# Two transformer blocks on one core: the first feed-forward layer takes its norm behind the product, and modulation tiles are sent by the pace of the weight chunks

## The reference, cut to what matters

```python
def modulate_pre(x, g_pre, shift, scale):
    return rms_norm(x, g_pre) * (1.0 + scale[:, None, :]) + shift[:, None, :]
def gated_post_add(x, y, g_post, gate, weight):
    return x + weight * gate[:, None, :] * rms_norm(y, g_post)
def swiglu_ffn(h, w_in, w_out):
    g, u = jnp.split(h @ w_in, 2, axis=-1)
    return (jax.nn.silu(g) * u) @ w_out
# per layer:  mod = silu(c) @ ada_w[layer] + ada_b[layer];  at the very end: rms_norm_2(x, final_norm)
```

## Time and profile before

| what | value |
|---|---|
| median of 3 runs | 2206.66 us (2205.58 to 2207.31) |
| profiled execution, its time | 2205.55 us |
| its span on the core | 2203.6 us |
| PE / DVE / ACT / POOL busy | 2112.3 / 1579.0 / 1004.5 / 192.0 us |
| mean granted clock of TensorE | 0.977 |
| transfers | 497 MB, 226 GB/s over the span |

### The profile page before, as it was taken

The page is one execution under the profiler, slowest core; times in us unless marked ns, Lnnn a source line. Parts: engine busy times, 40 slices in busy tenths (PEclk is TensorE's granted clock), DMA queues, the critical chain, the costliest instruction groups (busy, mean ns, idle before and its releaser), DMA issues.

```text
span 2203.6 us, 39291 instructions
## 1 busy us (share of the span) xinstructions
PE 2112.3 (96%) x17014; PEld 2062.3 (94%) x17014; DVE 1579.0 (72%) x1945; ACT 1004.5 (46%) x1073; POOL 192.0 (9%) x326
## 2 busy tenths in 40 slices
PE   5999999999999998799999999999999999999997
PEld 5999999999999997599998999999999899998997
DVE  6777887886767776778878464758888545757655
ACT  3344545434534444644445463346445445335442
POOL 0111101111011100010101000001111000000000
PEclk8999999999889998999999999999999999999999
DMA  8899474996479953068975555465996655555652
GB/s 327 288 315 331 165 253 153 319 343 249 153 246 324 320 184 134 2 218 275 346 261 174 180 184 191 153 231 173 359 370 203 194 182 189 166 173 201 210 187 100
DMA packets 265388, 497.39 MB, mean 226 GB/s; under 512 B 17152, under 2 KB 146560, under 8 KB 264832
## 3 DMA queue, kind: packets, MB, share of 16 engines
q1 hardware_dynamic: 230192, 366.42, 49.7%
q0 software_dynamic: 35024, 128.47, 15.8%
HBM read 491.68 MB, written 1.05 MB: 224 GB/s over the span
## 4 chain that ended last, share of the span: by engine, by line
PE 81%; DVE 10%; DMA 4%; ACT 3%; issue 2%; SPq 0%; DVEq 0%; POOL 0%; ACTq 0%
PE PA L494 8%; PE PA L496 8%; PE PA L495 8%; PE PB L494 7%; PE PB L496 7%; PE PB L495 7%; PE PY L494 7%; PE PY L496 7%; PE PY L495 7%; DVE wlo L1352 3%; ACT whi L994 1%; DMA raw<-ffn_w_in 1%; DVE opA_lo L1437 1%; PE PY L525 1%; DMA raw<-w_ff 1%
## 5 line engine op out<-in xcount | busy, mean ns | idle before, releaser
L1352 DVE TENSOR_TENSOR wlo<-raw,whi 128x2048 fp32r<-128x2048 f32 x335 | 766.7, 2299 | 366.9 <-ACT whi L994 366.2
L994 ACT ACTIVATE whi<-raw 128x2048 fp32r<-128x2048 f32 x335 | 636.7, 1907 | 485.0 <-DMA raw<-ffn_w_in 202.5
L494 PE MATMUL PA<-opA_hi,whi 128*128 128x256 f32 x1344 | 381.1, 284 | 9.0 <-DVE opA_lo L1402 7.3
L494 PE MATMUL PY<-opB_hi,whi 128*128 128x256 f32 x1344 | 377.5, 281 | 4.6 <-DVE wlo L1352 3.9
L496 PE MATMUL PA<-opA_hi,wlo 128*128 128x256 f32 x1344 | 379.2, 282 | 0.0
L495 PE MATMUL PA<-opA_lo,whi 128*128 128x256 f32 x1344 | 378.1, 281 | 0.0
L496 PE MATMUL PY<-opB_hi,wlo 128*128 128x256 f32 x1344 | 375.8, 280 | 0.0
L495 PE MATMUL PY<-opB_lo,whi 128*128 128x256 f32 x1344 | 375.6, 279 | 0.0
L494 PE MATMUL PB<-opA_hi,whi 128*128 128x256 f32 x1216 | 343.0, 282 | 1.0 <-DVE wlo L1352 1.0
L496 PE MATMUL PB<-opA_hi,wlo 128*128 128x256 f32 x1216 | 342.0, 281 | 0.0
L495 PE MATMUL PB<-opA_lo,whi 128*128 128x256 f32 x1216 | 341.0, 280 | 0.0
(11 more groups left out here) (307 smaller groups left out, 3532.6 us busy)
## 6 DMA issues: line engine op xcount, KB each, us to landing
raw<-ffn_w_in SPq DMA_DIRECT2D x176, 512.0 KB, 5.3
scr<-adat POOLq DMA_DIRECT2D x154, 512.0 KB, 6.3
raw<-w_in SPq DMA_DIRECT2D x144, 512.0 KB, 4.6
raw<-w_ff SPq DMA_DIRECT2D x128, 512.0 KB, 4.6
raw<-ffn_w_out SPq DMA_DIRECT2D x88, 512.0 KB, 4.7
adaw<-adat POOLq DMA_DIRECT2D x86, 512.0 KB, 6.3
raw<-w_branch SPq DMA_DIRECT2D x48, 512.0 KB, 4.4
raw<-a_w_in SPq DMA_DIRECT2D x24, 512.0 KB, 4.4
```

What stands on the lines that cost most here:

```text
L494: nc.tensor.matmul(o_, w1, rhs(xh), start=start, stop=False, skip_group_check=True)
L994: AC(whi[slot][:, 0:w], raw[slot][:, 0:w], ACT.Copy).then_inc(hi_ready, 1)
L1352: TT(wlo[slot][:, 0:w], raw[slot][:, 0:w], whi[slot][:, 0:w].bitcast(F32), ALU.subtract).then_inc(lo_ready, 1)
```

## The change

1. ffn00 takes the z form (`ffn("ffn00", ..., True)`, `widened("00")`, zhi/zlo from x directly, `acc_x("00")` on POOL). The norm of x ahead of it (`ssq`, `squares`, `inverse("00.x")`) goes. ScalarE starts pre before chunk 1's copy.
2. SP's first transfers: c, tiles 0 and 1, vec, base, tiles 2 to 5, x, chunk 0, tiles 6 to 15, chunk 1. The silu table is loaded by a dummy before c is there. VectorE splits chunk 0 after 12 tiles.
3. POOL sends a modulation tile when TensorE has finished the chunk three places ahead of the one at which VectorE is to reduce it (`ada_with`, `ffn_due`, `ff2_due`), not when a buffer comes free; `acc_x` of a seam stands ahead of the sends of the next stage in POOL's order.
4. Tiles per stage: cmp 12 in place of 8 (four of them already after chunk 87's split), nsa 4 in place of 8. ffn00 and ffn10 begin with their tiles at the third place of their order in place of the first.
5. The tables of the attention stage (five transfers, 0.7 MB) are issued in ffn01 ahead of chunk 62, not after its last chunk.
6. Last norm: VectorE adds four squares, TensorE sums the other four directly; ScalarE forms x*gain in `t10`; VectorE multiplies pairs of tiles by the factor (four instructions in place of eight).

The core of the diff:

```diff
-("cmp", 0, 8), ("ffn10", 24, 40), ("nsa", 32, 8)
+("cmp", 0, 12), ("ffn10", 24, 40), ("nsa", 32, 4)
+        def ffn_due(name, p):
+            rn, a_ = RUN[name][1], 3 if name in ("ffn00", "ffn10") else 5
+            return min(rn, max(0, p - a_ + 1) * rn // (FFN_AT["in", FFN_STEPS - 1] - a_))
+        def ff2_due(name, p):
+            rn = RUN[name][1]
+            return min(rn, max(0, p - 5) * rn // (FF2_AT["out", FF2_STEPS - 2] - 6))
...
 SP:
-                    first_ada(range(0, 13))
+                    if name == "ffn01" and (kind, j) == ("in", 5):
+                        sp.wait_ge(multiplied, CH["conv_out"] + 4)
+                        sp.dma_start(tnsa, I["t_nsa"]).then_inc(nsa_in, 16)
+                        sp.dma_start(pos2, I["cmp_pos2"]).then_inc(cmp_in, 16)
...
-                                first_ada(range(13, 16))
+                                first_ada(range(6, 16))
...
+            sp.dma_start(crow[:], I["c_rows"][0:1].partition_broadcast(P)).then_inc(crow_in, 16)
+            first_ada(range(0, 2))
             sp.dma_start(vec[:], I["vec"]).then_inc(vec_in, 16)
             sp.dma_start(base[:], I["t_base"]).then_inc(base_in, 16)
+            first_ada(range(2, 6))
             sp.dma_start(x[:], I["x_fm"]).then_inc(x_in, 16)
...
 TensorE:
                     need(pe, "V", "fin.acc")
                     nc.tensor.matmul(PB[:, 0, :], onesD, accx[:], start=True, stop=False)
+                    for k in range(4, KT):
+                        need(pe, "S", f"fin.sq{k}")
+                        last = nc.tensor.matmul(PB[:, 0, :], onesD, tmp8[:, k, :], start=False, stop=k == KT - 1)
...
-            ssq("00.x")
-            for f in range(9, 16):
+            for f in range(8, 17):
                 pe.wait_ge(ada_used, f)
                 idle(6)
             need(pe, "V", "first.mod")
-            idle(14)
-            ffn("ffn00", "00", False)
+            idle(8)
+            ffn("ffn00", "00", True)
...
 ScalarE:
+                    for k in range(KT):
+                        if k == 4:
+                            root("fin")
+                        S(AC(t10[:, k, :], x[:, k, :], ACT.Copy, scale=V("final", k, 1)), f"fin.g{k}")
...
+            S(AC(warm[:], epsc[:], ACT.Silu))
             act.wait_ge(crow_in, 16)
             S(AC(crow[:], crow[:], ACT.Silu), "csil0")
+            load_table(ACT.Sqrt)
+            prep_to(1)
             act.wait_ge(x_in, 16)
-            squares("00.x", x, lambda q: None)
-            root("00.x")
-            prep_to(2)
-            pre("00", tmp8)
+            need(act, "V", "first.mod")
+            for k in range(KT):
+                S(AC(oph["A"][:, k, :], x[:, k, :], ACT.Copy, scale=A_("00")[:, k:k + 1]), f"00.zhi{k}")
+                if k == 3:
+                    prep_to(2)
+            for k in range(KT):
+                S(AC(tmp8[:, k, :], x[:, k, :], ACT.Square), f"00.sq{k}")
+            prep_to(3)
...
 VectorE:
             for f in range(16):
-                if f == 9:
-                    inverse("00.x")
-                if f == 13:
+                if f == 12:
                     prep_to(1)
                 ada_to(f + 1)
             mods("first")
+            widened("00")
+            for k in range(KT):
+                need(dve, "S", f"00.zhi{k}")
+                S(STT(opl["A"][:, k, :], x[:, k, :], A_("00")[:, k:k + 1], oph["A"][:, k, :].bitcast(F32), ALU.mult, ALU.subtract),
+                  f"00.zlo{k}")
+                if k == 3:
+                    prep_to(2)
...
+            ada_to(RUN["cmp"][0] + 4)
...
-            ada_to(nsa0 + 2)
...
-            ada_to(nsa0 + 4)
...
-                    for k in range(KT):
-                        S(STT(tmp8[:, k, :], x[:, k, :], V("final", k, 1), rstd[:], ALU.mult, ALU.mult), f"fin.t{k}")
+                    for q in range(4):
+                        need(dve, "S", f"fin.g{2 * q + 1}")
+                        S(TT(tmp8[:, 2 * q:2 * q + 2, :], t10[:, 2 * q:2 * q + 2, :], rstd[:].unsqueeze(1).broadcast_to([P, 2, T]),
+                             ALU.mult), f"fin.t{q}")
...
 POOL:
-            ada_send(sum(RUN["ffn00"]) + SLABS)
+            def ada_with(name, due, last):
+                c0, r0 = CH[name], RUN[name][0]
+                for p in range(last + 1):
+                    if r0 + due(name, p) > sent[0]:
+                        pool.wait_ge(multiplied, c0 + max(1, p - 3))
+                        ada_send(r0 + due(name, p))
+            acc_x("00")
+            ada_ffn("ffn00")
             acc_x("01")
-            ada_send(sum(RUN["conv"]) + SLABS)
+            for i in range(4):
+                pool.wait_ge(multiplied, CH["conv_in"] + (3, 4, 7, 8)[i])
+                ada_send(RUN["conv"][0] + 2 * i + 2)
...
+            for i in range(6):
+                pool.wait_ge(multiplied, CH["kv"] + 1 + i)
+                ada_send(RUN["cmp"][0] + 2 * i + 2)
+            ada_ffn("ffn10")
             acc_x("11")
+            pool.wait_ge(multiplied, CH["nsa_in"] + 4)
             ada_send(nsa0 + 2)
...
-                ada_send(RUN[f"ff{l}"][0] + SLABS)
                 acc_x(f"b{l}1")
-                ada_send(sum(RUN[f"ff{l}"]))
+                ada_with(f"ff{l}", ff2_due, FF2_AT["out", FF2_STEPS - 2])
```

More of the change, by code:

```diff
@@ L294, in build @@
         ADA0, RUN, _n = {}, {}, 0
-        for _name, _count, _run in (("first", 16, 16), ("ffn00", 24, 40), ("conv", 24, 8), ("ffn01", 40, 40), ("cmp", 0, 8),
-                                    ("ffn10", 24, 40), ("nsa", 32, 8), ("ffn11", 40, 40), ("ff0", 48, 48), ("ff1", 8, 8)):
+        for _name, _count, _run in (("first", 16, 16), ("ffn00", 24, 40), ("conv", 24, 8), ("ffn01", 40, 40), ("cmp", 0, 12),
+                                    ("ffn10", 24, 40), ("nsa", 32, 4), ("ffn11", 40, 40), ("ff0", 48, 48), ("ff1", 8, 8)):
             ADA0[_name] = (_n, _count)
@@ L568, in out1024 @@
                     out_rows(c + q, (2 * q, 2 * q + 1), op, 2 * q, q == 0, q == 3, tag if q == 3 else None)
-            def ssq(tag, gap=0):
-                take("B")
-                for k in range(KT):
-                    if k % 2 == 0:
-                        if k:
-                            idle(gap)
-                        need(pe, "S", f"{tag}.sq{k // 2}")
-                    last = nc.tensor.matmul(PB[:, 0, :], onesD, tmp8[:, k, :], start=k == 0, stop=k == KT - 1)
-                S(last, f"{tag}.ssq")
-                by("B", "S", f"{tag}.sd")
             def idle(n):
@@ L999, in prep_to @@
                     nxt[0] += 1
-            def squares(tag, src, wait, own=None):
-                if own:
-                    need(act, "S", own)
-                for q in range(4):
-                    wait(q)
-                    S(AC(tmp8[:, 2 * q:2 * q + 2, :], src[:, 2 * q:2 * q + 2, :], ACT.Square), f"{tag}.sq{q}")
             def root(tag):
@@ L1426, in zevac, with widened @@
                     S(TS(zb[:], zb[:], scale, None, ALU.mult), f"{name}.z")
+            def widened(nsub):
+                own(S(nc.vector.tensor_copy(wide[:, :, T:T + 1], B_(nsub).unsqueeze(2))))
+                S(TT(wide[:, :, T + 1:ZC], B_(nsub).unsqueeze(2), wide[:, :, T:T + 1].bitcast(F32), ALU.subtract))
             def boundary(sub, nsub, c_done, c_next):
@@ L1831, in _ @@
             out_split(15)
-            ada_to(nsa0 + 8)
+            ada_to(sum(RUN["nsa"]))
             mods("nsa")
@@ L2010, in _ @@
             acc_x("12")
-            ada_send(sum(RUN["ffn11"]))
+            ada_ffn("ffn11")
             acc_x("b00")
```

61 lines of the change are left out of this document (24 added, 37 removed).

## The result

The median is 2188.77 us of four runs (2187.19 to 2190.43), before 2206.12 of four (2205.47 to 2207.31): ratio 0.9913, interval 0.9895 to 0.993, so 17.4 us faster where 22.1 were forecast. The profiled execution took 2188.2 with a span of 2186.2; of before 2205.55 with 2203.6.

What follows compares the result with a forecast made beforehand. TensorE, busy 2112.3 of 2203.6 us, was taken as the bound, so only its pauses and low-clock stretches could be won. Terms summed to -22.1, taking the median 2206.66 to 2184.6 us; range 2177 to 2194.

Steps and rivals of the forecast that it cites:

- Seam to kv: Tables moved into ffn01 shorten the seam into kv to the first seam's length: net -3.4 us, bounds 0 and -3.7.
- ff0 and ff1: Seams to these stages: paced tiles end a late chunk landing, so x starts earlier; together -8.0 us, bounds -3 and -10.
- Rival C: Bursts are not what makes x late at the second block's seams, which give 2 to 3; 2189.5 us, chance 0.13.
- End: Last norm: earlier last x and root, four double products in place of eight; -2.2 us, bounds -0.5 and -2.5.
- Start: ffn00: first matmul 6.3 us earlier at 38.8, chunk 0 faster by 1.4; -7.7 us, bounds -5 and -9.
- A: Whole kernel: the summed terms hold within 5 us, 2180 to 2190 us; chance 0.50.
- rival B: Kernel start pays 3 to 5 only, as tile 15 or the sum of squares is late; 2188 us, chance 0.14.
- B's second mechanism: Kernel start: POOL's sum of squares comes late, additions losing 2.2 to a split by the lock; L546 1.7 us late.
- cmp: Four tiles ahead of the block copies delay the split of chunk 88; +1.5 us, bounds 0 and +5.
- D: In cmp, tiles delay three splits and the half-clock stretch grows, losing 4 to 8; 2190 us, chance 0.10.
- nsa: Two tile reductions leave the chain ending in TensorE's wait of 8.69; -2.3 us, bounds -1 and -4.
- Rival G: Full stretches: paced tiles land too late and stop VectorE, so the kernel is slower; 2214 us at 0.2 per chunk, chance 0.04.

Runs made afterwards that it cites:

- experiment 3: Changed kernel with the five attention-table transfers issued after ffn01's last chunk again, as in the kernel before; 2190.11 us, ratio 0.9926.
- experiment 7: Changed kernel with GpSimd again sending six tiles ahead of its sum of squares for kv, tables staying in ffn01; one run of 2192.5 us.
- experiment 4: Changed kernel with GpSimd again sending six tiles at once ahead of its sums of squares at ff0 and ff1; 2198.64 us, ratio 0.9961.
- experiment 1: Changed kernel with ScalarE forming ffn00's eight squares of x early, while it waits for modulation tiles; 2192.71 us, ratio 0.9934.
- experiment 2: Changed kernel with cmp's first four tiles reduced in VectorE's idle stretch ahead of kv's second readout; 2187.23 us, ratio 0.9912.

## Why the prediction was right, and where it was off

The direction, the range and most places came out. Against the terms, from the columns:

**Seam to kv** (-3.4): -3.7. The size was right. The reason given, the tables, fell: with the tables late again the seam stays short (experiment 3), as it does with the burst again (experiment 7). That the two together made the 10.52 is the explanation left, and it is argued and not shown. The 0.3 put down for the tables in ffn01 does not appear: column 81 is 0.0.

**ff0 and ff1** (-8.0): -3.6 and -4.5. The first x starts right behind its product and L556 has no more than 0.5 of wait. The changed kernel is 5.4 ahead there, so its x at 1476.11 and L556 at 1486.60 stand for 1481.5 and 1492.0, where 1481.6 and 1492.2 were reckoned. At ff1 the 1.7 reckoned for matmuls at a slower pace behind the pause is the stretch from 2009.1 to 2012.5 at 0.50 (16 matmuls in 3.4 us), which is gone. Rival C is out; experiment 4 gives the same size from the other side.

**End** (-2.2): -2.1. Counted from the last chunk's end, the root begins at 3.2 in place of 5.0 (2178.24 - 2175.03, 2195.27 - 2190.31), and the products take 2.50 in place of 3.25. Of these 2.5, 2.1 reach the end.

**Start** (-7.7): -5.8, between A and rival B (3 to 5), by B's second mechanism. The first matmul came 5.9 earlier where 6.3 were reckoned, and chunk 0 took 1.5 less where 1.4 were; from the end of chunk 1 (50.94) on, chunk 2 took 7.6 in place of 5.7. So the mis-sized step is the sum of squares: 1.22 of wait, and 0.68 for its four small matmuls on TensorE, which the prediction put at nothing.

"First matmul at 38.8" against 39.24 is close by luck, for two errors cancel. The data stood at 37.2, 1.6 sooner than reckoned (the last tile was reduced by 35.45 and not 36.8), and I had not counted the unread matmuls of L583 as a queue of their own, which held the first real one 2.0 longer. The "seven additions on POOL at 0.86" that "end at about 50.3" ended at 52.01, though the first began at 41.92 and not at 44.3. The 0.86 of the seam holds for four of the six additions behind the first; the two that met a split of 128x2048 took 2.66 and 2.59, and no such split lies beside the first five at the seam. B reckoned with one such split; two were met, and the early beginning paid for the other. And I had read the 2.82 of one split as a small slowing. It is 2.29 and one addition of 0.53. The Trainium skill ("SBUF — State Buffer", section "SBUF: two separate sides") says of the two engines that "the other fully blocks"; by that rule, experiment 1's step of 1.67 is 1.15 for the tile and an estimated 0.52 for the addition behind it, and the trace agrees. No run takes the z form (change 1) or the order of the first transfers (change 2) by itself, so how the gain of the start divides between them is not shown.

**cmp** (+1.5, bounds 0 and +5): +4.1. The failed step is "its end moves from 580.93 to about 585.5, and 1.0 is lost". The split was indeed 0.9 late; TensorE waited longer for PA. The last copy ended at 582.2 before, 2.3 ahead of TensorE; delayed by 4.6 it gives the 2.2 that were measured. The pause was followed by an earlier and longer half-clock stretch, 41.0 for 37.5, which makes up the rest; with the pause gone (experiment 2) so is the loss. This is D at its lower edge, and in six other executions without an edit here the stretch was 44.3 and the loss 5.8.

**nsa** (-2.3): the wait fell by 2.3 (8.69 to 6.40), the stage by 1.5 in this execution.

**Not forecast:** +1.5 in ffn11, where nothing was edited. The changed kernel and the version with the old last norm have the same wait at the same place, 1.98 and 1.97; for the second, its stretch from the wait on follows:

```profile
999.05 0.36 PE L504 MATMUL PY<-opB_hi,whi 128*128 128x256 f32 x1 [1.98 <-DVE wlo L1353]
```

```profile
995.57 0.35 PE L504 MATMUL PY<-opB_hi,whi 128*128 128x256 f32 x1 [1.97 <-DVE wlo L1348]
```

```profile
995.60:1004.60 9.00, 9.00 (x76) 9.00 (x77) 7.19 (x7) 7.16 (x6) 0.00 (x0) 1.00 0.65 225
```

Behind it the changed kernel has the stretch from 999.5 to 1002.9 at a granted clock of 0.50, the version with the old norm has 1.00 throughout, and so has the kernel before, also with a wait of 1.98. Eight of the thirteen changed versions have such a stretch there, and these are the eight with +1.5 to +2.4 in the column. So the extra time is the clock's; why it falls behind the same wait in one execution and not in another, these runs do not show. And -1.5 in mix1: the kernel before waits 1.56 at 1728.77 for a split (chunk 259), the changed one 0.04 at the same place. Why that split was late is not shown either.

The sum of the columns is the measured 17.4; of the 4.7 that are missing, cmp has 2.6, the start 1.9, nsa 0.8, and the rest cancels. Rival G is out: 425 matmuls in 50 us.

## What to carry to other kernels

A wait that is removed shows the next one, and in a start with several chains (data, filler matmuls, a sum on another engine, a transfer behind a burst) none of the edits that were tried alone gained anything that its median shows: one read 1.5 us faster, the other two 2.5 and, in a single run, 5 slower. Together, with the tiles sent earlier, they gave 11. When work is inserted ahead of other work, look for every resource that the delayed work frees, the bank that it reads as well as the result that it makes. Put extra work where the engine's own idle time stands in the profile, and judge by the ends of chunks rather than by medians when the spread is as large as the effect.
